# The softmax bias taken directly as a minimum, and handed over head by head, in a two-layer streaming encoder

## The chip, the cores and the metric

The kernel runs on one core of one Trainium2 chip, as one program. The metric is the device time of one execution in microseconds; the time of a kernel is the median of its runs.

## The reference, cut to what matters

The reference computes two layers of an encoder for 512 rows of a prompt and 8 streams of 16 frames each (five row tiles of 128). In each layer a combined projection gives queries, keys, values and the inputs of an indexer and of a gated unit. The indexer's scores choose the keys that each row may attend to (128 of them for the prompt, 68 for the streams); attention is a softmax over the chosen keys. Then come the gated unit, a merge, an output projection and a mixture of experts. The change sits in the attention's softmax:

```python
_, sel = lax.top_k(score, topk)
valid = sel < limit[None, :, None]
...
logits = jnp.einsum('bqhgd,bqkhd->bqhgk', q, k_sel).astype(jnp.float32) * (HEAD_DIM ** -0.5)
logits = jnp.where(valid[:, :, None, None, :], logits, -jnp.inf)
p = jax.nn.softmax(logits, axis=-1).astype(v_sel.dtype)
o = jnp.einsum('bqhgk,bqkhd->bqhgd', p, v_sel)
```

HEAD_DIM is 64, so the scale is one eighth.

## The kernel before, in words

The program is written engine by engine: each of PE (TensorE), ACT (ScalarE), DVE (VectorE), POOL (GpSimd) and SP runs a hand-ordered list and waits on counting semaphores. Everything is fp32.

**Attention** runs over 40 units per layer (a unit is one head of one row tile: 8 heads of each of the four prompt tiles, then 8 units of the stream tile), taken two at a time as 20 pairs, p = 0 to 19. Pairs 0 to 15 are the prompt's (keys per row tile 128, 256, 384, 512), pairs 16 to 19 the streams' (272 keys). For a pair the steps are:

1. PE `logits(p)` (L918; L920 and L921 for the streams, where the mask is added by a matmul) writes two PSUM banks.
2. DVE `masked_logits(p)` (L1680): for each head one operation adds the mask `score(t)` to the logits, writes the sum to `probs` (tile `scr`), and takes its row maximum into `mx`. It is followed by a read of the accumulator, which the trace shows as a row of its own. After both heads DVE waits for itself and multiplies the two maxima by -1/8 into `nmx` (L1688, a TENSOR_SCALAR on 128x2); its end is signalled as `p_raw`, one count for the pair.
3. ACT `exps` (L1304): exponential of `probs` with bias `nmx` and scale 1/8, row sum into `den`, once for each head, signalled as `p_exp`.
4. DVE `roots(p)` (L1693): one reciprocal of both sums (128x2), after both exponentials. For the stream pairs two more operations (L1698) spread the last columns. One count of `rden_ready` for the pair.
5. ACT `normalise` (L1310) scales each head, PE transposes it (L934), ACT copies the transposes out (`probs_out`, L1320), PE multiplies by the values (L947, L958, L969), and ACT `tile_out` (L1324) stores a finished row tile.

The order of the work is written out by hand. On PE, each p runs `logits(p + 2)`, the transposes of p, a third of a projection job (`fill`, L781, in the first 15 pairs) and the values of p - 1. On ACT, each p runs `probs_out` of pair p - 1, `normalise` of p and `exps` of p + 1. On DVE, each p runs `roots(p)`, `masked_logits(p + 1)`, rounds of key selection, and one step of layer-norm statistics:

```python
for p in range(NAP):
    roots(p)
    if p + 1 < NAP:
        masked_logits(p + 1)
    for t in (2, 3, PT):
        select(t, p)
    if p == ROUNDS[PT][0] + len(ROUNDS[PT][1]) - 1:
        dve.wait_ge(dve_chain, last[PT])
        V.nop().then_inc(stream_scores, 1)
    if p < 2 * NT:
        ln_step(p)
```

A selection round (`step`, L1462) is a MAX8, a MATCH_REPLACE8 and in the last round of a tile a MEMSET (for the streams) and a TENSOR_SCALAR that turns the marks into a mask. The table ROUNDS gives row tile 3 two rounds in each of the pairs 2 to 9, and the stream tile 1, 1, 2, 2, 2, 1 rounds in the pairs 8 to 13. After the last of them, at p = 13, DVE signals `stream_scores`, for which PE waits ahead of `logits(16)`, the first stream pair.

The tenth `ln_step`, at p = 9, signals `ln_stat`. POOL waits for it, and then normalises the gated unit's rows: a power (L542, L545), five TENSOR_SCALARs (L639) and ten TENSOR_TENSORs (L643), all 128x512, in place. PE needs their results for `gating` after the first projection (L748) that follows attention.

Of the kernel before, what the change touches and what calls it, by code (L numbers as in the profile page):

```python
# [17 lines left out]
ALU = mybir.AluOpType  # L18
# [3 lines left out]
P = 128  # L22
DEPTH, D = 2, 1024
SEQ, STREAMS, FRAMES, PAST = 512, 8, 16, 256
PT = SEQ // P
# [77 lines left out]
def filled(i, L, e):  # L103
# [3 lines left out]


PER_LAYER = dict(
    rden_ready=20, u_ready=5, ks_rep_done=2, turned_idx=5, unit_done=16, rows_sent=1, sq_done=5, x_new=5,  # L110
    rs_ready=5, xt_psum=20, xt_done=20, proj_psum=25, proj_free=25, rope_done=5, rep_done=7, kx_psum=7, kx_done=5,
    qis_done=2, idx_psum=32, idx_relu=32, idx_used=32, qk_psum=5, qk_done=5, s_psum=40, p_raw=20, p_exp=40,
    p_ready=40, pt_psum=40, pt_done=40, pv_done=20, stream_scores=1, o_psum=5, o_done=5, ks_psum=8, ks_done=6, qts_done=2,
    ln_stat=1, ln_rs=1, ln_done=15, swm_ready=2, sw_psum=2, sw_done=2, sg_psum=5, sg_used=5, sgt_psum=5,
    sgt_done=5, mg_gate=10, mg_proj=10, mg_sig=10, mg_done=10, mt_psum=10, mt_done=10, xo_psum=10, xo_done=10,
# [37 lines left out]
def build(nc, a, o):  # L153
    ctx = ExitStack()
    with ctx:
# [37 lines left out]
        ss, rs = stat[:, 0:5], stat[:, 5:10]  # L193
        ss1, rs1 = stat[:, 100:105], stat[:, 105:110]
        rs_wide = stat[:, 110:110 + NT * (XW - D)].rearrange("p (t c) -> p t c", t=NT)
        mx, nmx, den, rden = (stat[:, 60 + PBUF * i:60 + PBUF * (i + 1)] for i in range(4))
        moments = stat[:, 18:28].rearrange("p (t c) -> p t c", c=2)
        lrs = stat[:, 28:33]
        half = stat[:, 33:38]
# [515 lines left out]
        def _(pe):  # L715
# [22 lines left out]
            for L in range(DEPTH):  # L738
# [168 lines left out]
                def logits(p):  # L907
                    t = TILE_OF[p]
                    if p >= 2:
                        pe.wait_ge(p_raw, prior("p_raw", L) + p - 1)  # L910
                    if p == NPP:
                        pe.wait_ge(stream_scores, prior("stream_scores", L) + 1)
                    for n in (2 * p, 2 * p + 1):
                        t, j, g = ATT_UNITS[n]
                        out = banks[LBANK[n % 4]][:, 0:KEYS[t]]
                        if t < PT:
                            r = slice(HD * g, HD * g + HD)
                            mm = pe.matmul(out, qt[r, j, t * P:(t + 1) * P], kt[r, 0:KEYS[t]], start=True, stop=True)  # L918
                        else:
                            pe.matmul(out, qts[g][:, j, :], qkv[:, j, SK0[g]:SK0[g] + KEYS[t]], start=True, stop=False)  # L920
                            mm = pe.matmul(out, rows_of[:, j, :], score(PT), start=False, stop=True)  # L921
                        mm.then_inc(s_psum, 1)
# [288 lines left out]
        def _(act):  # L1211
# [9 lines left out]
            for L in range(DEPTH):  # L1221
# [78 lines left out]

                def exps(n):
                    t, k = ATT_UNITS[n][0], n % PBUF
                    act.wait_ge(p_raw, prior("p_raw", L) + n // 2 + 1)
                    act.activation(probs[k][:, 0:KEYS[t]], probs[k][:, 0:KEYS[t]], ACT.Exp,  # L1304
                                   bias=nmx[:, k:k + 1], scale=ATT_SCALE, accum_out=den[:, k:k + 1]).then_inc(p_exp, 1)

                def normalise(n):
                    t, k = ATT_UNITS[n][0], n % PBUF
                    act.wait_ge(rden_ready, prior("rden_ready", L) + n // 2 + 1)
                    act.activation(probs[k][:, 0:KEYS[t]], probs[k][:, 0:KEYS[t]], ACT.Copy,  # L1310
                                   scale=rden[:, k:k + 1]).then_inc(p_ready, 1)

# [101 lines left out]
        def _(dve):  # L1414
# [188 lines left out]
            for L in range(DEPTH):  # L1603
# [66 lines left out]
                def masked_logits(p):  # L1670
# [3 lines left out]
                    for h in range(2):  # L1674
                        n = 2 * p + h
                        dve.wait_ge(s_psum, prior("s_psum", L) + n + 1)
                        if n >= PBUF:
                            dve.wait_ge(pt_psum, prior("pt_psum", L) + n - PBUF + 1)
                        raw = banks[LBANK[n % 4]][:, 0:KEYS[t]]
                        ins = V.tensor_tensor_reduce(out=probs[k + h][:, 0:KEYS[t]], in0=raw,  # L1680
                                                     in1=score(t) if t < PT else zero[:, :].broadcast_to([P, KEYS[PT]]),
                                                     scale=1.0, scalar=NEG, op0=ALU.add, op1=ALU.max,
                                                     accum_out=mx[:, k + h:k + h + 1])
                        if h == 0:
                            ins.then_inc(dve_chain, 1)
                            count[0] += 1
                    then(ins)
                    V.tensor_scalar(nmx[:, k:k + 2], mx[:, k:k + 2], -ATT_SCALE, None, ALU.mult).then_inc(p_raw, 1)  # L1688

                def roots(p):  # L1690
                    t, k = TILE_OF[p], 2 * p % PBUF
                    dve.wait_ge(p_exp, prior("p_exp", L) + 2 * p + 2)
                    ins = V.reciprocal(rden[:, k:k + 2], den[:, k:k + 2])  # L1693
                    if t == PT:

                        then(ins)
                        for h in range(2):
                            ins = V.scalar_tensor_tensor(probs[k + h][:, 3 * P:4 * P].rearrange("p (b i) -> p b i", b=STREAMS),  # L1698
                                                         over(probs[k + h][:, PAST:PAST + FRAMES], STREAMS, 1, [P, STREAMS, FRAMES]),
                                                         rden[:, k + h:k + h + 1],  # L1700
                                                         own_of[:, ATT_UNITS[2 * p + h][1], :].unsqueeze(2).broadcast_to([P, STREAMS, FRAMES]),
                                                         ALU.mult, ALU.mult)
                    ins.then_inc(rden_ready, 1)

                turn_rows(PT)
                select(1, -2)
# [181 lines left out]
```

## Time and profile before

| | us |
|---|---|
| median of 3 runs | 1461.88 |
| lowest and highest run | 1460.96, 1463.17 |
| profiled execution: its span, first to last instruction | 1460.0 |
| PE busy in the span | 1317.7 (90%) |
| DVE busy | 541.5 (37%) |
| ACT busy | 341.8 (23%) |
| POOL busy | 221.8 (15%) |
| attention of layer 0 | about 157 to 255 |
| attention of layer 1 | about 867 to 968 |

Of the profiled execution only its span is recorded, not the time of the whole launch; it lies 1.9 us below the median, so a change of the span is carried over to the median as a difference. The "granted clock" is the share of TensorE's full clock that the chip gave: 1.00 is 2.4 GHz and 0.50 is 1.2 GHz. In the rows, times of a single instruction in a timeline are in us, start first. Starts of successive DVE rows may overlap by some 0.1 us. A name after "<-" in square brackets is what ended the engine's idle time.

### The profile page before, as it was taken

What the parts mean: (1) busy time and instruction counts of PE and PEld (TensorE: products, weight loads), DVE (VectorE), ACT (ScalarE), POOL (GpSimd) and SP (SyncE); (2) the same over time, 40 slices, a digit from 0 to 9 for tenths busy, and PEclk for the clock granted to TensorE, in tenths of its full rate; (3) what the DMA queues carried; (4) which work ended last, traced back from release to release, by engine and by line L of the source; (5) the groups of instructions that cost most, each with busy time, mean ns of one, the idle gap of its engine ahead of it and who ended that gap; (6) DMA issues with size and microseconds to landing.
All of it is one profiled execution on the core that took longest, in us unless ns stands there. A gap on an engine that the chain in (4) does not pass through costs nothing.

```text
span 1460.0 us, 15494 instructions
## 1 busy us (share of the span) xinstructions
PE 1317.7 (90%) x5756; PEld 728.0 (50%) x5756; DVE 541.5 (37%) x1542; ACT 341.8 (23%) x773; POOL 221.8 (15%) x304
## 2 busy tenths in 40 slices
PE   7999898999999997988699989899999999979780
PEld 6654345544444555655474544464444445556550
DVE  1278885110111137212435779731011103452115
ACT  2232466200000100212213236551000010012121
POOL 5011033000000001223331200600000000013313
PEclk9999999999999997999899999999999999979995
DMA  8302102503303305999661210052060060289966
GB/s 238 115 13 59 58 1 71 173 1 87 129 0 142 146 29 190 397 404 369 236 151 65 62 60 1 8 157 80 0 216 0 0 259 40 78 295 412 406 247 238
DMA packets 95484, 205.62 MB, mean 141 GB/s; under 512 B 26464, under 2 KB 35904, under 8 KB 95408
## 3 DMA queue, kind: packets, MB, share of 16 engines
q1 hardware_dynamic: 80800, 178.13, 34.4%
q0 software_dynamic: 14608, 26.49, 5.2%
q8 instruction: 47, 0.77, 0.2%
q14 instruction: 29, 0.24, 0.0%
HBM read 196.29 MB, written 27.78 MB: 153 GB/s over the span
## 4 chain that ended last, share of the span: by engine, by line
PE 79%; DVE 6%; issue 4%; ACT 4%; DMA 4%; PEld 1%; POOL 1%; PEldq 1%; POOLq 0%; SPq 0%; ACTq 0%; DVEq 0%
PE bank L748 34%; PE bank L1030 10%; PE bank L1081 9%; PE bank L1127 7%; PE bank L1138 4%; PE bank L781 2%; PE bank L1114 2%; DMA uv<-xd,mb 2%; DVE stat L1688 1%; PE bank L830 1%; PE bank L1047 1%; PE bank L734 1%; DVE x L1822 1%; PE bank L834 1%; PE bank L1122 1%
## 5 line engine op out<-in xcount | busy, mean ns | idle before, releaser
L748 PE MATMUL bank<-ring,xt 128*128 128x512 f32 (+1 forms) x1120 | 433.6, 544 | 7.0 <-DMA ring<-in_w_in 4.2
L748 PEld LDWEIGHTS bank<-ring,xt 128*128 128x128 f32 x1120 | 213.7, 193 | 208.9 <-issue 190.2
L1757 DVE TENSOR_TENSOR scr<-scr,bank 128x512 f32<-128x512 f32 x20 | 13.7, 687 | 368.6 <-PE bank L1030 368.6
L1081 PE MATMUL bank<-ring,xt 128*128 128x512 f32 x320 | 141.3, 594 | 0.0
L542 POOL TENSOR_SCALAR stat<-stat 128x1 f32<-128x1 f32 (+1 forms) x27 | 11.3, 420 | 800.1 <-ACT uv L1214 615.2
L1358 ACT ACTIVATE scr<-bank,stat 128x512 f32<-128x512 f32 x40 | 25.3, 683 | 347.9 <-PE bank L748 347.9
L1081 PEld LDWEIGHTS bank<-ring,xt 128*128 128x128 f32 x320 | 59.3, 190 | 67.0 <-issue 67.0
L1030 PE MATMUL bank<-ring,att 128*128 128x512 f32 x160 | 72.5, 596 | 2.2 <-ACT sgt L1350 1.8
L781 PE MATMUL bank<-ring,xt 128*128 128x512 f32 x160 | 73.8, 594 | 0.0
L1030 PE MATMUL bank<-ring,sgt 128*128 128x512 f32 x160 | 71.9, 592 | 0.0
L748 PE MATMUL bank<-more,xt 128*128 128x512 f32 x160 | 70.3, 592 | 0.0
L1797 DVE TENSOR_TENSOR xt<-bank,gain 128x512 f32<-128x512 f32 x68 | 43.8, 685 | 66.4 <-PE bank L1114 66.4
L1127 PE MATMUL bank<-ring,xt 128*64 128x256 f32 x480 | 67.4, 388 | 0.2 <-issue 0.2
L1462 DVE MAX8 stat<-mb 128x8 f32<-128x256 f32 (+3 forms) x114 | 61.5, 540 | 3.0
L1462 DVE MATCH_REPLACE8 mb<-stat,mb 128x256 f32<-128x256 f32 (+3 forms) x114 | 59.7, 524 | 0.0
L1804 DVE SCALAR_TENSOR_TENSOR xt<-bank,uv,xt 128x128 f32<-128x128 f32 x34 | 11.9, 350 | 128.6 <-ACT xt L1379 128.6
L677 POOL DMA_INDIRECT yd<-scr,mb x34 | 34.1, 1002 | 166.2 <-ACT scr L1388 160.5
L1114 PEld LDWEIGHTS bank<-ident,uv 128*128 128x128 f32 x272 | 35.3, 196 | 31.9 <-issue 19.6
L934 PE MATMUL bank<-ident,scr 128*128 128x128 f32 x208 | 35.3, 293 | 17.0 <-ACT scr L1310 16.7
L1030 PEld LDWEIGHTS bank<-ring,att 128*128 128x128 f32 x160 | 29.9, 190 | 41.4 <-issue 39.1
L1768 DVE TENSOR_TENSOR x<-x,bank 128x512 f32<-128x512 f32 x20 | 13.7, 687 | 97.6 <-PE bank L1081 97.6
L1127 PEld LDWEIGHTS bank<-ring,xt 128*64 128x64 f32 x480 | 40.2, 139 | 19.5 <-issue 4.2
(285 smaller groups left out, 1839.3 us busy)
## 6 DMA issues: line engine op xcount, KB each, us to landing
ring<-in_w_in SPq DMA_DIRECT2D x12, 2048.0 KB, 9.3
ring<-in_w_ed SPq DMA_DIRECT2D x32, 512.0 KB, 18.2
ring<-in_w_eg SPq DMA_DIRECT2D x26, 512.0 KB, 10.0
ring<-in_w_eu SPq DMA_DIRECT2D x26, 512.0 KB, 17.6
ring<-in_w_out SPq DMA_DIRECT2D x4, 2048.0 KB, 12.4
more<-in_w_ed SPq DMA_DIRECT2D x14, 512.0 KB, 11.3
qkv<-in_w_eg SPq DMA_DIRECT2D x12, 512.0 KB, 6.7
qkv<-in_w_eu SPq DMA_DIRECT2D x12, 512.0 KB, 9.9
```

The source lines that it names most:

```text
L677: pool.indirect_dma_start(out=yd, in_=yout[z], in_offset=None, out_offset=bass.IndirectOffsetOnAxis(ap=index(b, 1, q), axis=0), bounds_che ...
L748: mm = pe.matmul(out, xt[:, k, t * P:(t + 1) * P], rhs[:, k, :], start=(k == 0), stop=(k == KD - 1))
L781: mm = pe.matmul(banks[7][:, :], xt[:, k, t * P:(t + 1) * P], rhs[:, k, :], start=(k == 0), stop=(k == KD - 1))
L934: mm = pe.transpose(banks[2 + n % 2][:, i * P:(i + 1) * P], probs[n % PBUF][:, c * P:(c + 1) * P], idm)
L1030: mm = pe.matmul(b[2 + half_][:, :], src[:, j, t * P:(t + 1) * P], w[:, 4 * half_ + j, :], start=(j == 0), stop=(j == 3))
L1081: mm = pe.matmul(banks[5 + n % 3][:, :], xt[:, k, t * P:(t + 1) * P], w[:, k, :], start=(k == 0), stop=(k == KD - 1))
L1114: mm = pe.transpose(banks[first + k // 4][:, (k % 4) * P:(k % 4 + 1) * P], xin[q][:, k:D:KD], idm)
L1127: mm = pe.matmul(banks[2 + z][BR * h:BR * h + BR, 0:2 * P].rearrange("p (m f) -> p m f", m=2), xin_t[z][:, k, BR * h:BR * h + BR], w[:, :, ...
L1138: mm = pe.matmul(banks[4 + c][BR * h:BR * h + BR, :], hidden_t[z][:, BR * h:BR * h + BR], two[h][1][c] if two[h] is places[PLACES - 1] els ...
L1358: ins = act.activation(scr[:, c0:c0 + 512], banks[4 * (n % 2) + m][:, :], ACT.Sigmoid, scale=rs1[:, n % NT:n % NT + 1])
L1462: make(*args, **kwargs).then_inc(dve_chain, 1)
L1797: V.tensor_tensor(xin_t[z][:, 4 * hf:4 * hf + 4, :], banks[first + hf][:, :].rearrange("p (k r) -> p k r", k=4), gain[:, L, 1, 4 * hf:4 * ...
```

## The change

`masked_logits` now asks the same kind of operation for (logits + mask) times -1/8, and for the row minimum of that, starting from +3.3e38: this is the bias itself, so `mx`, the wait of DVE for itself and the TENSOR_SCALAR on 128x2 are gone. The exponential takes scale -1.0. Each head's operation signals `p_raw`, and ACT waits for each head apart; PE waits for twice the count. `roots` takes the two reciprocals apart (128x1), each after its own exponential, and signals `rden_ready` for each head.

```diff
-        mx, nmx, den, rden = (stat[:, 60 + PBUF * i:60 + PBUF * (i + 1)] for i in range(4))
+        nmx, den, rden = (stat[:, 60 + PBUF * i:60 + PBUF * (i + 1)] for i in range(3))
...
-                        pe.wait_ge(p_raw, prior("p_raw", L) + p - 1)
+                        pe.wait_ge(p_raw, prior("p_raw", L) + 2 * (p - 1))
...
-                    act.wait_ge(p_raw, prior("p_raw", L) + n // 2 + 1)
+                    act.wait_ge(p_raw, prior("p_raw", L) + n + 1)
                     act.activation(probs[k][:, 0:KEYS[t]], probs[k][:, 0:KEYS[t]], ACT.Exp,
-                                   bias=nmx[:, k:k + 1], scale=ATT_SCALE, accum_out=den[:, k:k + 1]).then_inc(p_exp, 1)
+                                   bias=nmx[:, k:k + 1], scale=-1.0, accum_out=den[:, k:k + 1]).then_inc(p_exp, 1)
...
-                    act.wait_ge(rden_ready, prior("rden_ready", L) + n // 2 + 1)
+                    act.wait_ge(rden_ready, prior("rden_ready", L) + n + 1)
...
-                        ins = V.tensor_tensor_reduce(out=probs[k + h][:, 0:KEYS[t]], in0=raw,
-                                                     in1=score(t) if t < PT else zero[:, :].broadcast_to([P, KEYS[PT]]),
-                                                     scale=1.0, scalar=NEG, op0=ALU.add, op1=ALU.max,
-                                                     accum_out=mx[:, k + h:k + h + 1])
-                        if h == 0:
-                            ins.then_inc(dve_chain, 1)
-                            count[0] += 1
-                    then(ins)
-                    V.tensor_scalar(nmx[:, k:k + 2], mx[:, k:k + 2], -ATT_SCALE, None, ALU.mult).then_inc(p_raw, 1)
+                        V.tensor_tensor_reduce(out=probs[k + h][:, 0:KEYS[t]], in0=raw,
+                                               in1=score(t) if t < PT else zero[:, :].broadcast_to([P, KEYS[PT]]),
+                                               scale=-ATT_SCALE, scalar=-NEG, op0=ALU.add, op1=ALU.min,
+                                               accum_out=nmx[:, k + h:k + h + 1]).then_inc(p_raw, 1)

                 def roots(p):
                     t, k = TILE_OF[p], 2 * p % PBUF
-                    dve.wait_ge(p_exp, prior("p_exp", L) + 2 * p + 2)
-                    ins = V.reciprocal(rden[:, k:k + 2], den[:, k:k + 2])
-                    if t == PT:
-
-                        then(ins)
-                        for h in range(2):
+                    for h in range(2):
+                        dve.wait_ge(p_exp, prior("p_exp", L) + 2 * p + h + 1)
+                        ins = V.reciprocal(rden[:, k + h:k + h + 1], den[:, k + h:k + h + 1])
+                        if t == PT:
+                            then(ins)
                             ins = V.scalar_tensor_tensor(probs[k + h][:, 3 * P:4 * P].rearrange("p (b i) -> p b i", b=STREAMS),
...
-                    ins.then_inc(rden_ready, 1)
+                        ins.then_inc(rden_ready, 1)
```

The order on PE and ACT is unchanged. On DVE, an ordinary prompt pair (here the statistics step of pair 6, `roots(7)`, `masked_logits(8)`; ISA is the masked logits' operation and, in the row after it, its accumulator read) before:

```order
L1693 RECIPROCAL stat<-stat 128x2 [waits p_exp,dve_chain]
L1680 ISA scr,stat<-bank5,mb 128x256 [waits pt_psum,s_psum]
L1680 ISA stat 128x1
L1680 ISA scr,stat<-bank6,mb 128x256 [waits pt_psum,s_psum]
L1680 ISA stat 128x1
L1688 TENSOR_SCALAR stat<-stat 128x2 [waits dve_chain]
L1462 MAX stat<-mb 128x8 [waits dve_chain]
L1462 MATCH_REPLACE mb<-stat,mb 128x512 [waits dve_chain]
```

and now:

```order
L1689 RECIPROCAL stat<-stat 128x1 [waits p_exp,dve_chain]
L1689 RECIPROCAL stat<-stat 128x1 [waits p_exp]
L1680 ISA scr,stat<-bank5,mb 128x256 [waits pt_psum,s_psum]
L1680 ISA stat 128x1
L1680 ISA scr,stat<-bank6,mb 128x256 [waits pt_psum,s_psum]
L1680 ISA stat 128x1
L1462 MAX stat<-mb 128x8 [waits dve_chain]
L1462 MATCH_REPLACE mb<-stat,mb 128x512 [waits dve_chain]
```

One instruction that waited for DVE itself went, one that waits for ACT came. The second place is p = 13, with the last selection round of the stream tile between `masked_logits(14)` and `roots(14)`. Before:

```order
L1680 ISA scr,stat<-bank1,mb 128x512 [waits pt_psum,s_psum]
L1680 ISA stat 128x1
L1688 TENSOR_SCALAR stat<-stat 128x2 [waits dve_chain]
L1462 MAX stat<-mb 128x8 [waits dve_chain]
L1462 MEMSET stat 128x4 [waits dve_chain]
L1462 MATCH_REPLACE mb<-stat,mb 128x272 [waits dve_chain]
L1462 TENSOR_SCALAR mb<-mb 128x272 [waits dve_chain]
L1693 RECIPROCAL stat<-stat 128x2 [waits dve_chain,p_exp]
```

and now:

```order
L1680 ISA scr,stat<-bank1,mb 128x512 [waits pt_psum,s_psum]
L1680 ISA stat 128x1
L1462 MAX stat<-mb 128x8 [waits dve_chain]
L1462 MEMSET stat 128x4 [waits dve_chain]
L1462 MATCH_REPLACE mb<-stat,mb 128x272 [waits dve_chain]
L1462 TENSOR_SCALAR mb<-mb 128x272 [waits dve_chain]
L1689 RECIPROCAL stat<-stat 128x1 [waits dve_chain,p_exp]
L1689 RECIPROCAL stat<-stat 128x1 [waits p_exp]
```

The first of the two TENSOR_SCALARs between the masked logits and the reciprocal is gone; the second, which closes the selection and stands ahead of the `stream_scores` signal, stays.

## Rows read from the trace of the kernel before

**Rows 1.** The chain that ended last, in order of time (start us, us, what).
```profile
219.83 9.82 DVE stat L1688
...
929.53 9.84 DVE stat L1688
```

**Rows 2.** Busy time by stretch, us: PE, PEld, DVE, ACT, POOL, granted clock, DMA share, GB/s.
```profile
157.00:205.00 48.00, 42.05 (x194) 19.27 (x195) 43.99 (x142) 29.39 (x91) 0.00 (x0) 1.00 0.14 45
231.00:255.00 24.00, 21.25 (x204) 16.48 (x204) 8.55 (x40) 20.31 (x51) 2.35 (x3) 1.00 0.35 108
941.00:946.10 5.10, 5.10 (x15) 4.07 (x16) 1.90 (x8) 3.51 (x8) 0.00 (x0) 0.50 0.11 40
```

**Rows 3.** Who waited for whom, 157 to 205 us: us in total, times, longest.
```profile
DVE scr L1680 <- PE bank L918: 4.0, 1, 4.0
```

**Rows 4.** Timeline of DVE in pair 7: start us, us, operation, tiles, form.
```profile
184.64 0.17 DVE L1693 RECIPROCAL stat<-stat 128x2 f32<-128x2 f32 x1
184.76 0.42 DVE L1680 CUSTOM_DVE_ANT_0 scr<-bank,mb 128x256 f32<-128x256 f32 x1
185.11 0.08 DVE L1680 DVE_READ_ACCUMULATOR2_ANT stat<- 128x1 f32 x1
185.11 0.42 DVE L1680 CUSTOM_DVE_ANT_0 scr<-bank,mb 128x256 f32<-128x256 f32 x1
185.46 0.08 DVE L1680 DVE_READ_ACCUMULATOR2_ANT stat<- 128x1 f32 x1
...
185.65 0.69 DVE L1462 MAX8 stat<-mb 128x8 f32<-128x512 f32 x1
...
208.55 0.15 DVE L1693 RECIPROCAL stat<-stat 128x2 f32<-128x2 f32 x1
208.62 0.67 DVE L1680 CUSTOM_DVE_ANT_0 scr<-bank,mb 128x512 f32<-128x512 f32 x1
```

**Rows 5.** Timeline of POOL, 205 to 230 us.
```profile
205.35 0.20 POOL L542 TENSOR_SCALAR stat<-stat 128x5 f32<-128x5 f32 x1 [76.90 <-DVEq L1668]
207.03 10.32 POOL L639 TENSOR_SCALAR uv<-uv,stat 128x512 f32<-128x512 f32 x5
217.33 12.30 POOL L643 TENSOR_TENSOR uv<-uv,ring 128x512 f32<-128x512 f32 x10
```

**Rows 6.** Timeline of DVE, 209 to 231 us.
```profile
209.95 0.17 DVE L1688 TENSOR_SCALAR stat<-stat 128x2 f32<-128x2 f32 x1
210.02 0.44 DVE L1462 MAX8 stat<-mb 128x8 f32<-128x272 f32 x1
...
219.83 9.82 DVE L1688 TENSOR_SCALAR stat<-stat 128x2 f32<-128x2 f32 x1
229.57 0.43 DVE L1462 MAX8 stat<-mb 128x8 f32<-128x272 f32 x1
...
230.70 0.30 DVE L1462 TENSOR_SCALAR mb<-mb 128x272 f32<-128x272 f32 x1
```

**Rows 7.** Timelines of PE and ACT around the wait for the stream scores.
```profile
231.21 0.70 PE L920 MATMUL bank<-qkv,more 128*128 128x272 f32 x2 [2.98 <-DVEq L1738]
...
235.98 0.33 PE L947 MATMUL bank<-ring,qkv 128*64 128x128 f32 x2
...
940.92 1.25 PE L920 MATMUL bank<-qkv,more 128*128 128x272 f32 x2 [3.00 <-DVEq L1738]
948.55 1.09 PE L947 MATMUL bank<-ring,qkv 128*64 128x128 f32 x16
```

**Rows 8.** Groups of DVE by form, 157 to 255 us: count, busy us, mean ns, idle before.
```profile
L1680 DVE CUSTOM_DVE_ANT_0 scr<-bank,mb 128x512 f32<-128x512 f32 x8 | 5.2, 686 | 0.2 <-PE bank L934 0.2
L1462 DVE TENSOR_SCALAR mb<-mb 128x512 f32<-128x512 f32 x1 | 0.4, 427 | 0.0
```

**Rows 9.** Timeline of ACT in the stream pair 18.
```profile
247.88 0.86 ACT L1320 ACTIVATE ring<-bank 128x384 f32<-128x384 f32 x2
...
248.86 0.93 ACT L1310 ACTIVATE scr<-scr,stat 128x272 f32<-128x272 f32 x2
```

More of the change, by code:

```diff
@@ L109 @@
 PER_LAYER = dict(
-    rden_ready=20, u_ready=5, ks_rep_done=2, turned_idx=5, unit_done=16, rows_sent=1, sq_done=5, x_new=5,
+    rden_ready=40, u_ready=5, ks_rep_done=2, turned_idx=5, unit_done=16, rows_sent=1, sq_done=5, x_new=5,
     rs_ready=5, xt_psum=20, xt_done=20, proj_psum=25, proj_free=25, rope_done=5, rep_done=7, kx_psum=7, kx_done=5,
-    qis_done=2, idx_psum=32, idx_relu=32, idx_used=32, qk_psum=5, qk_done=5, s_psum=40, p_raw=20, p_exp=40,
+    qis_done=2, idx_psum=32, idx_relu=32, idx_used=32, qk_psum=5, qk_done=5, s_psum=40, p_raw=40, p_exp=40,
     p_ready=40, pt_psum=40, pt_done=40, pv_done=20, stream_scores=1, o_psum=5, o_done=5, ks_psum=8, ks_done=6, qts_done=2,
```

## The prediction

> **What bounds the kernel now.** I read the chain of waits first, since only work on it can move the end. It is nearly all PE, but it has one odd piece in each layer: a DVE TENSOR_SCALAR on 128x2, the very instruction that the change removes, with 9.82 and 9.84 us [rows 1]. Next I read the busy time by stretch. From 157 to 205 us DVE is busy 43.99 of 48 us [rows 2], and its one long wait there is 4.0 us at the start [rows 3]. So the first ten pairs of attention run at DVE's pace, with the key selection in between. From 231 to 255 us PE has 21.25 of 24 us and DVE 8.55 [rows 2]: there PE leads, and ACT in the last two pairs.
>
> The middle is set by neither. POOL starts when the tenth statistics step is done, at 205.35, and runs without a pause to 217.33 + 12.30 = 229.63 [rows 5]. DVE's TENSOR_SCALAR starts at 219.83 and ends at 229.65 [rows 6], with the last of POOL's ten TENSOR_TENSORs. The same instruction at 209.95, beside POOL's TENSOR_SCALARs, took 0.17 us [rows 6]. What waits behind the stalled one is the last selection round, after which DVE releases the stream scores; PE, which had run out of work 2.98 us before, starts the stream pairs at 231.21 [rows 7]. So a layer's attention is: DVE's pace up to the start of POOL, then a fixed 24.3 us of POOL, then what is left after the release.
>
> **The change part by part**, for one layer; it acts alike in both.
>
> *A. DVE up to the start of POOL.* Ten of the small TENSOR_SCALARs lie there behind a busy DVE (those of pairs 1 to 10; the one of pair 0 is hidden, DVE then waits for ACT anyway). From the second accumulator read at 185.46 to the MAX8 at 185.65 there are 0.19 us [rows 4]. An operation that waits for nothing starts with the accumulator read before it (both at 185.11), so up to 0.19 us can go; if MAX8 starts only at the end of the read (0.08), 0.11 go. Nine pairs (1 to 9) get a second reciprocal: a reciprocal takes 0.12 us to the next start (184.64 to 184.76), and at best 0.07 (208.55 to 208.62) [rows 4]. Ends: 10 x 0.11 - 9 x 0.12 = 0.0 us, and 10 x 0.19 - 9 x 0.07 = 1.3 us. I take the middle, **0.65 us**, since the rows lean to neither. Earlier exponentials buy nothing here: the reciprocals find them done, except in pair 0.
>
> *B. The release of the stream scores.* The stalled instruction goes, but the stall does not: between it and the release stands another TENSOR_SCALAR, on 128x272. That one reads and writes SBUF like the stalled one, and it takes 0.30 us for 272 elements [rows 6] and 0.43 for 512 [rows 8], so 0.13 us for 240 more, twice the pace of the masked-logits operation (686 ns for 512 [rows 8]). I expect it to start at about 221 us, inside POOL's TENSOR_TENSORs, and to wait for their end too. What goes off the path is the rest of the round (MAX8, MEMSET, MATCH_REPLACE8), now done during the stall. Before, the big TENSOR_SCALAR started at 230.70 and PE 0.51 us later, at 231.21 [rows 6, 7]. The stalled small one ended at 229.65, as if it had started at 229.65 - 0.17 = 229.48. A big one in its place brings PE to 229.48 + 0.51 = 229.99: **1.2 us** earlier. The ends are 0 (the whole round is held up) and 3.0 us (nothing is, and PE has no gap).
>
> *C. The two heads apart.* In the first ten pairs this is hidden by DVE, from the release to about 247 us by PE, which runs its list almost without a gap. In the last pairs ACT is on the path: its copy of pair 17 ends at 247.88 + 0.86 = 248.74, and the normalisation of pair 18 starts at 248.86, waiting for the roots [rows 9]. With the first head's root ready early, these 0.12 us go, and the same in pair 19: **0.25 us**, between 0 and 0.5.
>
> *Hidden.* The exponentials of pair 14 no longer wait for the stall, but nobody can use them: their reciprocals are queued on DVE behind the big TENSOR_SCALAR. PE's wait for twice the count, the scale -1.0 and the starting value cost nothing. No DMA moves; the stages behind start earlier with everything that they wait for.
>
> *Sum.* 0.65 + 1.2 + 0.25 = 2.1 us a layer, 4.2 us in all. The profiled span of 1460.0 us becomes 1455.8; it lies 1.9 us below the median of the runs, so the median goes from 1461.9 to **1457.7 us**.
>
> **A rule against the trace.** The trace shows a TENSOR_SCALAR of 0.17 us held for 9.8 us, across eight instructions of POOL of 12.30 / 10 = 1.23 us each, and another, at 209.95, that took its 0.17 us in the middle of a POOL instruction of 10.32 / 5 = 2.06 us [rows 5, 6]. The Trainium skill (SBUF — State Buffer, "Who interferes with whom") says that a VectorE operation in a two-port mode and a GpSimd instruction exclude each other on a shared port pair, and that whoever issues first holds it for its whole instruction. The cause fits; the duration does not: by that rule the wait would end with the one instruction in progress, and the change would fall to the first rival below.
>
> **The rivals.**
>
> *1. The big TENSOR_SCALAR gets through between two of POOL's instructions*, after at most 12.30 / 10 = 1.23 us. Then the stream scores are released at about 223 us, before PE has finished its earlier work, and PE's gap of 2.98 us [rows 7] closes: 3.0 + 0.25, and up to 0.65 more if PE was itself led by DVE, so 3.3 to 3.9 us a layer; and the clock does not fall (below), 2.9 us once. 9.4 to 10.7 us in all, about **1452 us**. Against it: the small one did not get in at any of the seven boundaries between them that it saw (9.82 / 1.23), nor in layer 1 [rows 1]. Chance 0.08.
>
> *2. The whole round is held up*, MAX8 or MATCH_REPLACE8 too. For it: neither is seen beside POOL's TENSOR_TENSORs. Against it: MAX8 took 0.44 us beside POOL's TENSOR_SCALARs and 0.43 after POOL's end [rows 6], and its pace is not doubled. Then B is 0: 2 x (0.65 + 0.25) = 1.8 us, **1460.1 us**, within 0.2%. Chance 0.12.
>
> *3. The clock.* In layer 1 the granted clock fell to 0.50, which is 1.2 GHz, during PE's gap, and stayed there from 941.0 to 946.1 [rows 2]. From the first stream matmul to the values of pair 13 it took 948.55 - 940.92 = 7.63 us there, and 235.98 - 231.21 = 4.77 in layer 0, where the clock held through an equal gap [rows 7]: a fall costs 2.9 us. The change shortens the gap from 3.0 to about 1.8 us, so a fall becomes less likely, not impossible. The forecast keeps one, as profiled. With none, 1457.7 - 2.9 = **1454.8 us**, chance 0.20; with one in each layer, 1460.6 us, chance 0.05.
>
> *4. Slower: the minimum form costs more than the maximum form.* The place is again the first half, where DVE has no spare time: 20 of these operations lie ahead of POOL's start. The gain of 2.1 us a layer is gone when each takes 2.1 / 20 = 0.1 us more, and the kernel is slower by 0.2% (2.9 us) from 0.18 us on. Were it to run at half the pace, a 256-wide one (0.42 us [rows 4]), about the mean width up to pair 10, would take some 0.27 more (256 elements at 686 - 420 = 266 ns for 256 [rows 4, 8]); 20 x 0.27 = 5.4 us a layer, and 2 x (5.4 - 2.1) = 6.6 us in all make **1468.5 us**. Against it: the maximum form already carries a scale (of 1.0), so both forms add, scale and compare. Chance 0.04.
>
> That the change doesn't do what it says: the instructions go as described, so only its effect is open. Nothing else that I can name holds more than 0.01.
>
> **How the numbers follow.** The forecast has 0.51; its own range is 1456.4 (A at 1.3) to 1459.0 (A at 0), and 0.7 us more on both sides for the measurement, since the three runs lie up to 1.3 us from their median. The range for all leaves out rival 1 below and rival 4 above, 0.12 together, and takes in the case without a fall and the whole of rival 2: 1453.5 to 1461.2 us. 0.2%, about what a measurement of this kernel can tell from no change, is 2.9 us: 1459.0. Faster by more: 0.43 of the forecast, the case without a fall 0.20, rival 1 0.08, and 0.01 of rival 2: 0.72. Slower by more (above 1464.8, or near it): 0.04. The rest is 0.24.
>
> **What would show it.** The chain should have a DVE piece of 8 to 9 us again, now on L1462, with a TENSOR_SCALAR on 128x272 that starts near 220 us and ends at POOL's end. POOL should start at about 204.7 instead of 205.35 (A), PE's first stream matmul should come 0.36 us behind POOL's end instead of 1.58 (B), and in pair 18 the normalisation should follow ACT's copy without 0.12 us between them (C). If POOL starts no earlier, A was nothing. If the 128x272 takes 0.30 us, rival 1 has it; if MAX8 takes 8 us, rival 2. A granted clock of 0.50 behind PE's gap tells how many falls there were.

## The result, and the profile after

| | before | changed |
|---|---|---|
| median of 4 runs, us | 1462.53 | 1452.99 |
| lowest and highest | 1460.96, 1463.17 | 1451.22, 1453.77 |
| span of the profiled execution | 1460.0 | 1451.5 |
| ratio of the runs | | 0.9932, 95% interval 0.9915 to 0.9949 |

The kernel became 9.5 us faster. 1457.7 was forecast, with a range from 1453.5: the direction was right, the size was not. The profiled execution of the changed kernel took 1453.34 us in all, so 1.8 us lie around its span.

The whole span is too coarse to find the gain in, as the stretch between two attentions varies by several microseconds between executions (last section). I count from the first logits matmul of a layer (L918, at 156.83 and 866.88 us before, at 157.97 and 864.52 after). All times in this table are us after it; they are differences of starts in the timelines.

| | before, layer 0 | layer 1 | changed, layer 0 | layer 1 |
|---|---|---|---|---|
| POOL starts (L542) | 48.52 | 48.17 | 46.62 | 46.27 |
| PE starts the stream logits | 74.38 | 74.04 | 71.30 | 70.95 |
| PE's gap ahead of them | 2.98 | 3.00 | 0.67 | 0.70 |
| the next stage starts (L748) | 98.39 | 100.91 | 94.74 | 94.38 |
| granted clock falls behind the gap | no | yes | no | no |

Attention is 3.65 us shorter in layer 0 and 6.53 in layer 1. The rest adds up: the first attention began 1.14 us later, the stretch between the attentions took 0.15 more and the end 0.39 more, so 8.5 us of span went.

The chain of waits of the changed kernel, in order of time (start, us, what), has its DVE piece still, on the other instruction:

```profile
221.23 7.84 DVE mb L1462
```

The timeline of DVE in pair 7 of the changed kernel, against [rows 4]:

```profile
184.65 0.22 DVE L1689 RECIPROCAL stat<-stat 128x1 f32<-128x1 f32 x2
184.79 0.41 DVE L1680 CUSTOM_DVE_ANT_0 scr<-bank,mb 128x256 f32<-128x256 f32 x1
185.12 0.08 DVE L1680 DVE_READ_ACCUMULATOR2_ANT stat<- 128x1 f32 x1
185.12 0.42 DVE L1680 CUSTOM_DVE_ANT_0 scr<-bank,mb 128x256 f32<-128x256 f32 x1
185.46 0.08 DVE L1680 DVE_READ_ACCUMULATOR2_ANT stat<- 128x1 f32 x1
185.46 0.69 DVE L1462 MAX8 stat<-mb 128x8 f32<-128x512 f32 x1
```

MAX8 starts with the second accumulator read, so the whole 0.19 us went. The two reciprocals together take 0.14 us to the next start, where the one took 0.12. The minimum form takes 0.41 and 0.42 us, the maximum form 0.42.

The timelines of POOL and DVE in layer 0 of the changed kernel, against [rows 5, 6]:

```profile
204.59 0.20 POOL L542 TENSOR_SCALAR stat<-stat 128x5 f32<-128x5 f32 x1 [75.00 <-DVEq L1668]
216.57 12.33 POOL L643 TENSOR_TENSOR uv<-uv,ring 128x512 f32<-128x512 f32 x10
```
```profile
220.09 0.44 DVE L1462 MAX8 stat<-mb 128x8 f32<-128x272 f32 x1
220.60 0.06 DVE L1462 MEMSET stat<- 128x4 f32 x1
220.77 0.42 DVE L1462 MATCH_REPLACE8 mb<-stat,mb 128x272 f32<-128x272 f32 x1
221.23 7.83 DVE L1462 TENSOR_SCALAR mb<-mb 128x272 f32<-128x272 f32 x1
229.21 0.23 DVE L1689 RECIPROCAL stat<-stat 128x1 f32<-128x1 f32 x2
```

MAX8, MEMSET and MATCH_REPLACE8 run at their usual pace beside POOL's TENSOR_TENSORs, and the 128x272 TENSOR_SCALAR is held up until these end at 216.57 + 12.33 = 228.90. PE starts the stream logits at 229.27, 0.37 us behind them; 0.36 was forecast.

The timeline of PE ahead of the stream logits in layer 0, before and changed, with the last work that PE has there:

```profile
227.13 1.09 PE L947 MATMUL bank<-ring,qkv 128*64 128x128 f32 x16
```
```profile
227.50 1.09 PE L947 MATMUL bank<-ring,qkv 128*64 128x128 f32 x16
229.27 0.70 PE L920 MATMUL bank<-qkv,more 128*128 128x272 f32 x2 [0.67 <-DVEq L1732]
```

The timeline of PE in layer 1 of the changed kernel, and busy time by stretch of the same (columns as in [rows 2]), against [rows 2, 7]:

```profile
933.67 1.09 PE L947 MATMUL bank<-ring,qkv 128*64 128x128 f32 x16
935.47 0.70 PE L920 MATMUL bank<-qkv,more 128*128 128x272 f32 x2 [0.70 <-DVEq L1732]
```
```profile
935.47:938.25 2.78, 2.78 (x16) 2.42 (x17) 1.58 (x7) 2.64 (x6) 0.60 (x1) 1.00 0.25 94
```

The gap is 0.70 us, not 1.8, the granted clock stays at 1.00 behind it, and the first matmul takes 0.70 us where it took 1.25.

The timeline of ACT in the stream pair 18 of the changed kernel, against [rows 9]:

```profile
245.94 0.87 ACT L1320 ACTIVATE ring<-bank 128x384 f32<-128x384 f32 x2
246.68 0.94 ACT L1310 ACTIVATE scr<-scr,stat 128x272 f32<-128x272 f32 x2
```

The normalisation starts 0.13 us before the copy's recorded end, where it had started 0.12 us behind it.

### The profile page after: what moved, and what is told of

It is laid out like the page before. It is cut to its first block, busy times and chain, and to the rows that moved or that the text cites. A ratio compares the mean times of both kernels' runs of the same rounds, so it can differ in the third digit from the quotient of the medians.

```text
span 1451.5 us, 15494 instructions
## 1 busy us (share of the span) xinstructions
PE 1316.5 (91%) x5756; PEld 729.4 (50%) x5756; DVE 534.1 (37%) x1542; ACT 339.4 (23%) x773; POOL 222.4 (15%) x304
## 4 chain that ended last, share of the span: by engine, by line
PE 79%; DVE 5%; DMA 4%; ACT 4%; issue 4%; PEld 1%; POOL 1%; PEldq 1%; SPq 0%; POOLq 0%; ACTq 0%; DVEq 0%
PE bank L748 34%; PE bank L1030 10%; PE bank L1081 10%; PE bank L1127 7%; PE bank L1138 4%; PE bank L1114 2%; PE bank L781 2%; DMA uv<-xd,mb 2%; DVE mb L1462 2%; PE bank L830 1%; PE bank L1047 1%; PE bank L734 1%; PE bank L834 1%; PE bank L1122 1%; PE bank L934 1%
## 5 line engine op out<-in xcount | busy, mean ns | idle before, releaser
L748 PE MATMUL bank<-ring,xt 128*128 128x512 f32 (+1 forms) x1120 | 434.0, 544 | 7.9 <-DMA ring<-in_w_in 5.1
L748 PEld LDWEIGHTS bank<-ring,xt 128*128 128x128 f32 x1120 | 214.3, 194 | 209.5 <-issue 190.0
L542 POOL TENSOR_SCALAR stat<-stat 128x1 f32<-128x1 f32 (+1 forms) x27 | 11.7, 434 | 796.2 <-ACT uv L1214 614.0
L748 PE MATMUL bank<-more,xt 128*128 128x512 f32 x160 | 70.3, 592 | 0.0
L1462 DVE MAX8 stat<-mb 128x8 f32<-128x256 f32 (+3 forms) x114 | 61.7, 541 | 3.0
L1462 DVE MATCH_REPLACE8 mb<-stat,mb 128x256 f32<-128x256 f32 (+3 forms) x114 | 59.7, 524 | 0.0
L748 PEld LDWEIGHTS bank<-more,xt 128*128 128x128 f32 x160 | 30.5, 190 | 38.2 <-issue 38.2
L1030 PEld LDWEIGHTS bank<-ring,sgt 128*128 128x128 f32 x160 | 30.4, 190 | 38.2 <-issue 38.2
```

Of the source, the lines that this page charges most:

```text
L748: mm = pe.matmul(out, xt[:, k, t * P:(t + 1) * P], rhs[:, k, :], start=(k == 0), stop=(k == KD - 1))
L1030: mm = pe.matmul(b[2 + half_][:, :], src[:, j, t * P:(t + 1) * P], w[:, 4 * half_ + j, :], start=(j == 0), stop=(j == 3))
L1462: make(*args, **kwargs).then_inc(dve_chain, 1)
```

## The experiments

The theory after the result: DVE's time ahead of POOL's start is worth 1.9 us a layer, the place of the stalled TENSOR_SCALAR 1.2, the hand-over by head some 0.5, and the fall of the clock behind PE's gap is the rest. The rivals were that the early hand-over carries the gain, and that the fall was chance. Unless said otherwise, "as after" means the changed kernel's numbers in the table above. The experiments were timed in several sets of runs, and the kernel before had a median of 1461.2 to 1463.1 us in them; a difference of medians between two sets is therefore good to 1 or 2 us only. Places inside a layer come from one profiled execution of each kernel.

**e1: the minimum without the hand-over by head**

```diff
-                    act.wait_ge(p_raw, prior("p_raw", L) + n + 1)
+                    act.wait_ge(p_raw, prior("p_raw", L) + n // 2 + 1)
...
-                                               accum_out=nmx[:, k + h:k + h + 1]).then_inc(p_raw, 1)
+                                               accum_out=nmx[:, k + h:k + h + 1])
+                    ins.then_inc(p_raw, 1)
...
-                        ins = V.reciprocal(rden[:, k + h:k + h + 1], den[:, k + h:k + h + 1])
+                    ins = V.reciprocal(rden[:, k:k + 2], den[:, k:k + 2])
```

> The changed kernel with the minimum form kept, but its end signalled once for a pair, and one 128x2 reciprocal for a pair, as before: only the small TENSOR_SCALAR and DVE's wait for itself are gone. Measured from the first logits of a layer, POOL started at 48.5 us before and at 46.6 after, and the next stage began at 98.4 (layer 0) before and at 94.7 after. Theory (the removed instruction gives the gain): POOL starts at 46.4 to 46.6, the 128x272 TENSOR_SCALAR is the one that stalls, the next stage begins at 94.9 to 95.3; the time is 0.3 to 1.2 us above the changed kernel. Rival (handing over head by head gives the gain): POOL starts at about 48.3 and the time is within 2 us of the kernel before.

Measured: 1454.02 us (ratio to before 0.9936, 0.9918 to 0.9955). POOL starts at 46.53 and 46.57 us, the stream logits at 71.25 and 71.26, the next stage at 95.17 and 95.18. So the removed instruction gives all of the first two terms. The hand-over by head gives what is left: from the stream logits to the next stage it takes 95.17 - 71.25 = 23.92 us in both layers, where it took 23.44 and 23.43 after, so 0.5 us a layer. The rival is out. The timeline of ACT in pair 18 of this kernel has the wait back:

```profile
246.37 0.87 ACT L1320 ACTIVATE ring<-bank 128x384 f32<-128x384 f32 x2
247.35 0.93 ACT L1310 ACTIVATE scr<-scr,stat 128x272 f32<-128x272 f32 x2
```

**e2: only the reciprocals by head**

```diff
-                    dve.wait_ge(p_exp, prior("p_exp", L) + 2 * p + 2)
-                    ins = V.reciprocal(rden[:, k:k + 2], den[:, k:k + 2])
+                    for h in range(2):
+                        dve.wait_ge(p_exp, prior("p_exp", L) + 2 * p + h + 1)
+                        ins = V.reciprocal(rden[:, k + h:k + h + 1], den[:, k + h:k + h + 1])
```

> The kernel before with nothing but the two reciprocals apart, each behind its own exponential and signalled by itself. Theory: POOL starts 0.0 to 0.4 us later than before (a second reciprocal costs about 0.02 us of DVE in each of nine pairs), the small TENSOR_SCALAR still stalls for 9.8 us, the tail gives 0.2 to 0.6 us a layer; the time is within 1.5 us of the kernel before. Rival (the hand-over by head gives half the gain or more): 4 to 5 us faster than before.

Measured: 1462.76 us, ratio 0.9998 (0.9985 to 1.0011): no change. POOL starts at 48.20 and 48.29 us, the small TENSOR_SCALAR stalls for 9.88. The next stage starts at 99.28 and 99.48, later than before in layer 0, since the clock fell at PE's gap (3.04 and 3.03 us) in both layers. The tail's gain is there all the same, behind the fall. The timeline of ACT in layer 0, and a stretch of busy time over the tail, at full clock again:

```profile
247.70 0.60 ACT L1324 ACTIVATE att<-bank 128x512 f32<-128x512 f32 x1 [2.22 <-PEq L973]
...
250.77 0.87 ACT L1320 ACTIVATE ring<-bank 128x384 f32<-128x384 f32 x2
251.51 0.94 ACT L1310 ACTIVATE scr<-scr,stat 128x272 f32<-128x272 f32 x2
```
```profile
236.00:257.00 21.00, 19.04 (x193) 14.73 (x193) 7.96 (x37) 15.82 (x43) 2.36 (x3) 1.00 0.37 110
```

The next stage (L748) starts 257.69 - 247.70 = 9.99 us after this `tile_out` of the last prompt tile. Counted in the same way it is 10.41 us before, 10.33 in e1 and 9.84 after. The reciprocals apart alone give 0.4 us a layer in the tail, inside the 0.2 to 0.6 that was expected.

**e3: the selection one pair earlier**

```diff
-ROUNDS = {1: (-2, [16]), 2: (-1, [12, 2, 2]), 3: (2, [2] * 8), PT: (8, [1, 1, 2, 2, 2, 1])}
+ROUNDS = {1: (-2, [16]), 2: (-1, [12, 2, 2]), 3: (2, [2] * 8), PT: (8, [1, 1, 2, 3, 2])}
```

> The changed kernel with the stream tile's last selection round moved one pair forward (rounds 1, 1, 2, 3, 2 from pair 8 on), so that its TENSOR_SCALAR on 128x272 comes ahead of POOL's TENSOR_TENSORs. Theory (it waits for these alone): it starts some 0.4 us before the first of them and takes 0.3 us, the stream scores are released some 12 us earlier, PE's gap of 0.67 us ahead of the stream logits closes, and a layer's attention gets 0.6 to 1.2 us shorter; 1 to 2.5 us faster than the changed kernel. Rival (PE or ACT lead there anyway, or the TENSOR_SCALAR is late and still stalls): within 0.5 us of the changed kernel.

Measured: 1457.4 us, 12 runs from 1449.76 to 1466.71, ratio 0.9955 (0.9932 to 0.9979), so 4 us slower than the changed kernel at the median. The profile shows both outcomes in one execution; the timelines of DVE and POOL, layer 0 and then layer 1:

```profile
217.18 12.42 DVE L1462 TENSOR_SCALAR mb<-mb 128x272 f32<-128x272 f32 x1
...
931.20 0.67 DVE L1462 TENSOR_SCALAR mb<-mb 128x272 f32<-128x272 f32 x1
```
```profile
217.16 12.28 POOL L643 TENSOR_TENSOR uv<-uv,ring 128x512 f32<-128x512 f32 x10
...
931.69 12.38 POOL L643 TENSOR_TENSOR uv<-uv,ring 128x512 f32<-128x512 f32 x10
```

In layer 0 it was 0.02 us late and waited for all ten. `masked_logits(14)` was queued behind it, PE stood for 6.98 us, the clock fell, and the next stage began at 103.18 us. In layer 1 it was 0.5 us early and took 0.67 us. PE then had no gap, as its timeline shows:

```profile
942.60 1.09 PE L947 MATMUL bank<-ring,qkv 128*64 128x128 f32 x16
943.63 0.73 PE L920 MATMUL bank<-qkv,more 128*128 128x272 f32 x2
```

The stream logits started at 70.19 us instead of 70.95 and the next stage at 93.65 instead of 94.38. So without the stall a layer is 0.7 us shorter, the size of PE's gap. Both theories had it half: the margin decides.

**e4: POOL's TENSOR_TENSORs replaced**

```diff
-                            ins = pool.tensor_tensor(v, v, (ln_g, ln_b)[step - 1], (ALU.mult, ALU.add)[step - 1])
+                            ins = pool.tensor_scalar(v, v, moments[:, t, 0:1], lrs[:, t:t + 1], ALU.subtract, ALU.mult)
```

> The changed kernel with POOL's ten TENSOR_TENSORs (the layer norm's gain and bias) replaced by the TENSOR_SCALAR of the step before them; the gain and the bias are left out of the result. POOL's 15 TENSOR_SCALARs of 2.06 us then end at 46.6 + 1.7 + 31.0 = 79.3 us from the first logits. Theory (DVE's two-port instruction is held up by the TENSOR_TENSORs only, as the small one ran in 0.17 us beside a TENSOR_SCALAR of POOL): the 128x272 TENSOR_SCALAR takes 0.3 to 0.8 us, PE has no gap, the attention of a layer is 0.6 to 1.2 us shorter than after. Rival (any instruction of POOL that uses SBUF holds it up until POOL pauses): it takes about 15 us, the stream logits start at 79.6 instead of 71.3 us, and the kernel is about 16 us slower than the changed one.

Measured: 1450.58 us (3 runs, 1447.94 to 1453.61), without the gain and bias. The timelines of DVE and POOL, layer 0:

```profile
219.62 0.30 DVE L1462 TENSOR_SCALAR mb<-mb 128x272 f32<-128x272 f32 x1
```
```profile
214.30 20.59 POOL L643 TENSOR_SCALAR uv<-uv,stat 128x512 f32<-128x512 f32 x10
```

The same instruction of DVE takes 0.30 us in the middle of POOL's TENSOR_SCALARs: it is POOL's TENSOR_TENSORs that hold it up. The second half of the expectation failed. With no stall, PE has no gap, but the stream logits start at 71.25 and 71.08 us and the next stage at 94.72 and 94.55, as after. That does not show that the stall costs nothing, as PE itself was late here. Early in both layers, some 3 to 7 us after the first logits, the clock stood at 0.50 for a while, and PE's work ahead of the stream logits ended 0.7 and 0.9 us later than after. Layer 0 of e9, the same kernel as after, shows that such an early fall makes PE late, by 0.4 us there (below); that it accounts for all of the 0.7 and 0.9 us here is not shown. Layer 1 of e3 is the one layer with neither the stall nor that fall, and there the stall was worth 0.7 us.

**e5: the small instruction put back**

```diff
                                                accum_out=nmx[:, k + h:k + h + 1]).then_inc(p_raw, 1)
+                    dve.wait_ge(p_raw, prior("p_raw", L) + 2 * p + 2)
+                    V.tensor_scalar(stat[:, 72:74], nmx[:, k:k + 2], -1.0, None, ALU.mult)
```

> The changed kernel with the small instruction put back where it cannot hold up anybody's data: behind each pair's minima, and after their signals, DVE waits for itself and multiplies nmx by -1 into two unused columns (TENSOR_SCALAR on 128x2). Theory (the 0.19 us of DVE for each such instruction ahead of POOL's start, ten of them, are 1.9 of the 3.7 us a layer; and the place of the stall decides 1.2 more): POOL starts 48.4 to 48.6 us after the first logits instead of 46.6, the small one stalls for some 9.8 us, the selection round comes behind it and the stream logits start at about 74.2 instead of 71.3; a layer's attention is 2.4 to 3.2 us longer than after, the kernel 5 to 7 us slower than the changed one, and a fall of the clock to 0.50 behind PE's gap of 3 us may come back. Rival (the gain comes from the bias being ready earlier, not from DVE's time): within 2 us of the changed kernel.

Measured: 1464.38 us (ratio 1.0015, 0.9999 to 1.0031), 11 us slower than the changed kernel. POOL starts at 48.19 and 48.27 us, the stream logits at 74.06 and 74.14, the next stage at 99.18 and 100.47. The timeline of DVE in layer 0, then that of PE in layer 1, then a stretch of busy time in layer 1:

```profile
221.11 9.77 DVE L1685 TENSOR_SCALAR stat<-stat 128x2 f32<-128x2 f32 x1
230.79 0.43 DVE L1462 MAX8 stat<-mb 128x8 f32<-128x272 f32 x1
```
```profile
947.43 1.24 PE L920 MATMUL bank<-qkv,more 128*128 128x272 f32 x2 [3.01 <-DVEq L1734]
```
```profile
949.20:953.30 4.10, 4.10 (x14) 3.32 (x14) 0.83 (x5) 1.12 (x4) 0.00 (x0) 0.50 0.00 0
```

It was expected to be 5 to 7 us slower than the changed kernel, and more if the clock fell. Nobody reads what this instruction writes, and yet the whole loss is back: 46.62 to 48.19 is the first term, 74.06 - 48.19 = 25.87 us from POOL's start to the stream logits against 71.30 - 46.62 = 24.68 is the second, and the clock falls in both layers, which adds 1.7 and 2.9 us behind the stream logits (99.18 - 74.06 = 25.12 and 100.47 - 74.14 = 26.33, against 23.44 and 23.43 after). The rival is out.

**e6: the gap opened again, and nothing else**

```diff
+                        for _ in range(3):
+                            step(PT, V.max, bests[PT - 1], mb[:, 640:1280])
                         dve.wait_ge(dve_chain, last[PT])
                         V.nop().then_inc(stream_scores, 1)
```

> The changed kernel with three more MAX8 over 640 columns (some 0.83 us each) between the last selection round and the signal of the stream scores; their results are not used. It delays the signal by 2.5 us and nothing ahead of it, so PE's gap is 3.2 us again. Theory (PE's gap of 3 us makes the granted clock fall in some layers, and a fall costs 1.7 to 2.9 us): each layer's attention is 2.3 to 2.5 us longer, and in one or both layers the clock falls to 0.50 behind the gap, which adds 1.7 to 2.9 us; 5 to 10 us slower than the changed kernel. Rival (the fall in layer 1 of the kernel before was chance and has nothing to do with the gap): 4.6 to 5 us slower, without a fall there.

Measured: 1460.62 us (ratio 0.9996, 0.998 to 1.0011), 7.6 us slower than the changed kernel. The stream logits start at 73.89 and 73.54 us, 2.6 later, as meant, and the clock falls behind the gap in both layers. The timeline of PE in layer 0, and a stretch of busy time just behind:

```profile
232.10 1.25 PE L920 MATMUL bank<-qkv,more 128*128 128x272 f32 x2 [3.25 <-DVEq L1734]
```
```profile
232.50:235.00 2.50, 2.50 (x7) 1.80 (x7) 1.19 (x5) 2.49 (x6) 0.00 (x0) 0.50 0.00 0
```

From the stream logits to the next stage it takes 98.79 - 73.89 = 24.90 and 98.55 - 73.54 = 25.01 us, against 23.44 and 23.43 after: each fall costs some 1.5 us here, where the one of [rows 7] cost 2.9. The difference goes with how long the clock stayed at 0.50: from 73.4 to 76.9 us after the first logits in layer 0 here, from 73.0 to 79.9 in the layer of [rows 7].

**e7: one element instead of two**

```diff
-                    V.tensor_scalar(nmx[:, k:k + 2], mx[:, k:k + 2], -ATT_SCALE, None, ALU.mult).then_inc(p_raw, 1)
+                        V.tensor_scalar(nmx[:, k + h:k + h + 1], mx[:, k + h:k + h + 1], -ATT_SCALE, None,
+                                        ALU.mult).then_inc(p_raw, 1)
```

> The kernel before with its maxima handed over head by head: for each head DVE waits for itself and multiplies one maximum (TENSOR_SCALAR on 128x1), two small instructions for a pair. Theory: each costs DVE 0.19 us and there are 10 more of them ahead of POOL's start, which comes at 50.2 to 50.5 us instead of 48.4. A single element a row leaves nothing to read through a second port, so if it is the two-port pace that stalls, the small ones take 0.17 us beside POOL's TENSOR_TENSORs and the selection's 128x272 stalls instead; the kernel is 2 to 5 us slower than before. Rival (any TENSOR_SCALAR of DVE stalls there, whatever its size): a 128x1 one stalls for 8 to 10 us, and the kernel is 5 to 8 us slower than before.

Measured: 1459.87 us (ratio 0.9986, 0.9967 to 1.0006), so not slower than before, against both expectations. POOL starts at 50.45 and 50.62 us. The timelines of DVE and POOL, layer 0:

```profile
223.85 0.15 DVE L1684 TENSOR_SCALAR stat<-stat 128x1 f32<-128x1 f32 x1
...
225.91 7.66 DVE L1462 TENSOR_SCALAR mb<-mb 128x272 f32<-128x272 f32 x1
```
```profile
221.11 12.30 POOL L643 TENSOR_TENSOR uv<-uv,ring 128x512 f32<-128x512 f32 x10
```

A 128x1 TENSOR_SCALAR takes 0.15 us beside POOL's TENSOR_TENSORs, where a 128x2 one took 9.8. POOL starts 2 us later than before, but the stream logits start only 0.7 and 1.3 us later (75.10, 75.29), since the stall is now behind the round, and PE's gap is 0.92 and 1.79 us. The clock fell behind the second of these.

**e8: the selection earlier, with a margin**

```diff
-ROUNDS = {1: (-2, [16]), 2: (-1, [12, 2, 2]), 3: (2, [2] * 8), PT: (8, [1, 1, 2, 2, 2, 1])}
+ROUNDS = {1: (-2, [16]), 2: (-1, [12, 2, 2]), 3: (2, [2] * 8), PT: (8, [1, 1, 2, 4, 1])}
```

> The changed kernel with rounds 1, 1, 2, 4, 1 of the stream tile from pair 8 on. In e3 the 128x272 TENSOR_SCALAR was queued at 57.8 us after the first logits in layer 1 and got through, and at 58.6 in layer 0, where POOL's TENSOR_TENSORs had just begun, and stalled for 12.4 us. With one round fewer in front of it there it comes at 56.6 to 57.7 in both layers, against POOL's 58.6. Theory (PE leads once nothing stalls, as in layer 1 of e3, where a layer's attention was 0.7 us shorter than after): both layers take 93.6 to 94.2 us, 0.5 to 2 us faster than the changed kernel, without e3's spread. Rival (the fourth round in pair 11 delays the pairs behind it by as much as the release gains): within 0.5 us of the changed kernel or slower.

Measured: 1452.87 us (6 runs, 1448.64 to 1454.08; ratio 0.9934, 0.9909 to 0.9959), the same as the changed kernel. The timeline of DVE, layer 0:

```profile
215.60 0.30 DVE L1462 TENSOR_SCALAR mb<-mb 128x272 f32<-128x272 f32 x1
```

It gets through in both layers, in 0.30 and 0.84 us, and the attentions take 94.43 and 94.70 us against 94.74 and 94.38. It doesn't beat the changed kernel, and no other kernel of this study does with the full result. As in e4, PE has no gap but is late itself, with the clock at 0.50 early in both layers, so this profile can't tell what the stall gone is worth; layer 1 of e3 says up to 0.7 us a layer.

**e9: the changed kernel again**

No edit.

> The changed kernel as it is, timed again, since the part of a layer behind attention varied between profiled executions by up to 7 us. Theory (3.7 us a layer, and 1 to 2 falls of the clock of 1.5 to 2.9 us less): 9 to 11 us faster than before, a layer's attention 94.3 to 94.8 us long, PE's gap 0.6 to 0.8 us, no fall of the clock behind it in either layer. Rival (the first measurement was lucky and the change is worth what was forecast): 4 to 6 us faster.

Measured: 1453.16 us, before 1462.23 beside it, ratio 0.9946 (0.9926 to 0.9967), 9.1 us. The attentions take 94.74 and 94.37 us, PE's gaps are 0.28 and 0.70 us, no fall behind them. In layer 0 the clock fell early; two stretches of busy time there, and PE's timeline ahead of the stream logits:

```profile
161.30:164.50 3.20, 3.04 (x5) 1.47 (x6) 3.10 (x11) 1.44 (x8) 0.00 (x0) 0.50 1.04 342
164.80:168.00 3.20, 3.20 (x13) 1.40 (x12) 3.06 (x13) 1.91 (x8) 0.00 (x0) 1.00 0.43 166
```
```profile
228.30 1.09 PE L947 MATMUL bank<-ring,qkv 128*64 128x128 f32 x16
229.68 0.70 PE L920 MATMUL bank<-qkv,more 128*128 128x272 f32 x2 [0.28 <-DVEq L1732]
```

PE's work ahead of the gap ends at 229.39 - 158.37 = 71.02 us after the first logits instead of 70.62, so 0.4 us later, while DVE releases the stream logits at the same time (71.31 against 71.30). So the early fall took its time out of PE's gap, and the layer is as long as after.

## Why the prediction was right or wrong

*What bounds.* Right, with the mechanism: the three parts of attention and the stall that moves instead of going. The chain named L1462, and the 128x272 TENSOR_SCALAR took 7.8 us to POOL's end.

*A, DVE up to POOL's start: mis-sized, and the largest error of a term.* Forecast 0.65 us, between 0.0 and 1.3; measured 48.52 - 46.62 = 1.90, and 48.17 - 46.27 = 1.90. Both prices came from the right rows, but were combined at the wrong ends. The removed slot is the full 0.19 us, since MAX8 starts with the read in front of it, as the next masked-logits operation was already seen to do in [rows 4]. The second reciprocal costs 0.02 us, not 0.07 to 0.12: I had priced it at a lone reciprocal's distance to a masked-logits operation. These prices give 10 x 0.19 - 9 x 0.02 = 1.7 us; the 0.2 us to the measured 1.90 is within what single layers differ by (POOL's start differs by 0.35 us between the two layers before, and e1, which has no second reciprocal, gained 1.99 and 1.60). e5 puts 1.6 to 2.0 us of it back.

*B, the release: right.* Forecast 1.2; measured (74.38 - 71.30) - 1.90 = 1.18 us, 1.19 in layer 1. The rival in which the whole round is held up is out by the rows after. The one in which the instruction slips between two of POOL's is out as well. e3 missed the first of ten by 0.02 us and waited for all. The 1452 us of that rival lie near the result by chance: its mechanism did not occur.

*C, the heads apart: small, as forecast, but twice the size.* Forecast 0.25; from the stream logits to the next stage it is 24.01 before and 23.44 after in layer 0, 0.57 us. Of these e1 gives 0.5 to the hand-over and leaves 0.1 to the removed instruction. The wait was the right one, but I counted it only up to the recorded end of ACT's copy. The normalisation of pair 18 went from 0.12 us behind that end to 0.13 ahead of it, 0.25 us for one pair, and pair 19 did the same (0.13 behind before, 0.13 ahead after).

*The clock: the step that failed, beside A.* I took the gap as 3.0 - 1.2 = 1.8 us and kept one fall. But A shortens the gap too: PE's own work ahead of it gained less than DVE did. PE is busy there but for 1.4 us of waits for ACT's normalisations between POOL's start and the gap, before and changed alike, and it ended only 0.77 us earlier (228.22 - 156.83 = 71.39 against 228.59 - 157.97 = 70.62), while the release came 3.08 earlier. So 2.98 - 3.08 + 0.77 = 0.67 us. I wrote that A shifts the release, and did not carry it into the gap. And one fall was less than the usual: of the eight gaps of 2.9 to 3.3 us in the profiles of before, e2, e5 and e6, seven had a fall behind them, and the profile I read showed the exception. Of the twelve layers with a gap of at most 0.92 us, or none, (after, e1, layer 1 of e3, e4, layer 0 of e7, e8, e9) none had one. e6 opens the gap again in the changed kernel and has a fall in both layers, so the link of gap and fall was tested, on two layers. A fall costs 1.5 to 2.9 us.

*The sum.* Per layer 1.9 + 1.2 + 0.6 = 3.7 us instead of 2.1, so 7.3 in all, and 2.9 for the fall in the profiled execution, is 10.2; 1.7 came back elsewhere in that pair of executions. Against the medians it is 9.5. The "no fall" case had its chance, 0.20, but on top of terms that were too small: 1454.8 where 1451.7 follows from the measured ones. The measured terms with one fall kept would give 1461.9 - 7.3 = 1454.6. So neither error alone explains the time; A, too small by 1.25 us a layer, and the gap, 1.8 us instead of 0.7, do so together. How many falls a typical execution of the kernel before has is not known: one profile of it was taken, with one.

*The slower case.* It did not happen: the minimum form takes 0.41 to 0.42 us for 256 columns and the maximum form 0.42.

*The rule.* The Trainium skill (SBUF — State Buffer, "Who interferes with whom") says that a VectorE operation in a two-port mode and GpSimd exclude each other on a shared port pair, and that the first holds it for its whole instruction. The runs agree with the exclusion for a 128x2 and a 128x272 TENSOR_SCALAR against POOL's TENSOR_TENSOR, and show no wait for a 128x1 one. They disagree on two points: the wait passes over seven boundaries and more between POOL's instructions, and it is not there against POOL's TENSOR_SCALAR (0.17 us before, 0.30 us in e4). The measurement decides.

## What to carry to other kernels

A stall in the chain belongs to the place in the queue as much as to the instruction: before removing it, look for the next instruction of the same kind behind the same neighbour, and price the way between the two. When a release moves, work out the gap of the engine behind it from both of its ends, and look at several layers or executions for what the clock does behind a gap of that size. A tiny instruction with a wait for its own engine costs its full slot on a saturated engine (0.19 us here, ten times ahead of POOL's start), however few elements it has.

## What the runs showed of the hardware

- DVE's TENSOR_SCALAR on SBUF with 2 or 272 fp32 elements a row waits for a run of POOL's ten TENSOR_TENSORs to end, not for one of them: 7.1 to 12.4 us. With one element a row it takes 0.15 us there (e7). Not held up there are MAX8 (0.44 us), MATCH_REPLACE8 (0.42), MEMSET (0.06), RECIPROCAL (0.17) and the masked-logits operation with one input in PSUM (0.69 for 512 columns).
- Beside POOL's TENSOR_SCALARs the same instruction takes 0.17 to 0.35 us (128x2) and 0.30 us (128x272). The 128x272 one took 0.67 us when it started 0.5 us ahead of the TENSOR_TENSORs (e3, layer 1), and 0.84 us when it started 0.7 us ahead (e8, layer 1).
- The granted clock fell to 0.50 at seven of eight gaps of PE of 2.9 to 3.3 us, at a price of 1.5 to 2.9 us each. It also fell at the one gap of 1.79 us (e7), where it cost 1.7 us, and at the one of 6.98 us (e3). It fell at none of the gaps of 0.92 us or less.
- The clock also fell some 3 us after the first logits in eleven of the 22 profiled layers; why was not looked into. In layer 0 of e9 POOL started no later for it (46.61 us against 46.62 after), but PE's work ahead of the stream logits ended 0.4 us later.
- The stretch from the end of one attention to the start of the next took from 608.9 to 615.8 us in the ten profiled executions before e9, with no relation to the edits in attention. What causes it was not looked into.
